# Old x loaded ahead of the last weights, old x pieces moved between jobs and end, column sums ahead of the cache transposes, plain weights split earlier

## The reference

```python
def swiglu_half(x, pre_g, w_gate, w_up, w_down, post_g):
    h = rms_norm(x, pre_g)
    u = jax.nn.silu(h @ w_gate) * (h @ w_up)
    return x + 0.5 * rms_norm(u @ w_down, post_g)

def run_layer(x, pos, token_mix, ff1, mix, ff2):
    x = swiglu_half(x, *ff1)
    mo, proj = mixer_projections(rms_norm(x, mix_pre_g), pos, w_in, ...)
    h_m, attn, new_state = token_mix(proj)      # mLSTM heads and latent attention
    ...
    x = x + rms_norm(merged @ w_out, mix_post_g)
    return swiglu_half(x, *ff2), new_state
```

## Time and profile before

| | |
|---|---|
| time, median of 3 runs | 1250.32 us (1250.29 to 1253.73) |
| the profiled execution | 1250.35 us, of which the span (first to last instruction) 1248.6 |
| TensorE matmuls busy | 1188.5 us (95%) |
| VectorE busy | 929.9 us (74%) |
| ScalarE busy | 639.2 us (51%) |
| GpSimd busy | 99.7 us (8%) |
| mean granted TensorE clock | 0.982 of 2.4 GHz |
| chain that ended last | PE 78%, DVE 11%, issue 4%, ACT 4%, DMA 2% |

### The profile page before, as it was taken

How to read it: one execution, slowest core, us unless ns; L and a number is a source line. 1 busy time by engine, 2 the same in 40 slices (tenths; PEclk the granted TensorE clock), 3 DMA queues, 4 the chain that set the end, 5 groups by cost and what they waited for, 6 DMA issues and landing times.

```text
span 1248.6 us, 22101 instructions
## 1 busy us (share of the span) xinstructions
PE 1188.5 (95%) x8460; PEld 1126.8 (90%) x8460; DVE 929.9 (74%) x1394; ACT 639.2 (51%) x1250; POOL 99.7 (8%) x128
## 2 busy tenths in 40 slices
PE   6999999999989999999998999999999999999877
PEld 6999999999989799999965679989999999999876
DVE  7988999899888734644357551279889998998856
ACT  5565655565555423132266443345666555655544
POOL 2000000000000003604034001110000000000000
PEclk8999999999999899999999999999999999999989
DMA  8224224313323312423200001232242243133222
GB/s 254 69 68 136 68 84 121 102 56 115 102 76 131 90 51 68 92 55 91 76 14 24 24 1 35 68 110 68 69 135 69 85 119 102 59 112 102 77 102 76
DMA packets 162549, 104.72 MB, mean 84 GB/s; under 512 B 16907, under 2 KB 160352, under 8 KB 161936
## 3 DMA queue, kind: packets, MB, share of 16 engines
q1 hardware_dynamic: 161344, 101.50, 28.2%
q0 software_dynamic: 1088, 1.84, 0.5%
q10 hardware_dynamic: 16, 0.00, 0.0%
HBM read 95.06 MB, written 8.27 MB: 83 GB/s over the span
## 4 chain that ended last, share of the span: by engine, by line
PE 78%; DVE 11%; issue 4%; ACT 4%; DMA 2%; SPq 0%; DVEq 0%; POOL 0%; ACTq 0%
PE PS L641 43%; PE PS L391 17%; PE PS L683 4%; ACT WQ_HI L740 3%; PE PS L409 2%; PE PS L2250 2%; PE PS L2221 2%; DVE SB L787 2%; PE PS L2236 1%; DMA RAWP<-in_ff_w_up 1%; DVE TU L866 1%; DVE SB L791 1%; DVE UF L1068 1%; PE PS L1944 1%; PE PS L1596 1%
## 5 line engine op out<-in xcount | busy, mean ns | idle before, releaser
L641 PE MATMUL PS<-HHI,WQ_HI 128*128 128x288 f32 x1120 | 332.8, 297 | 8.0 <-ACT SNQ L722 3.9
L641 PE MATMUL PS<-HLO,WQ_HI 128*128 128x288 f32 x1120 | 331.1, 296 | 0.0
L641 PE MATMUL PS<-HHI,WQ_LO 128*128 128x288 f32 x1120 | 330.0, 295 | 0.0
L641 PEld LDWEIGHTS PS<-HHI,WQ_HI 128*128 128x128 f32 x1120 | 210.2, 188 | 10.9 <-ACT WQ_HI L740 6.6
L740 ACT ACTIVATE WQ_HI<-SB 128x512 fp32r<-128x512 f32 (+2 forms) x288 | 163.9, 571 | 105.2 <-PE PS L641 60.2
L641 PEld LDWEIGHTS PS<-HHI,WQ_LO 128*128 128x128 f32 x1120 | 211.2, 189 | 0.0
L641 PEld LDWEIGHTS PS<-HLO,WQ_HI 128*128 128x128 f32 x1120 | 210.4, 188 | 0.0
L641 PE MATMUL PS<-UHI,WQ_HI 128*128 128x288 f32 x616 | 187.2, 304 | 11.8 <-DVE ULO L853 9.3
L641 PE MATMUL PS<-ULO,WQ_HI 128*128 128x288 f32 x616 | 184.3, 299 | 0.0
L641 PE MATMUL PS<-UHI,WQ_LO 128*128 128x288 f32 x616 | 184.3, 299 | 0.0
L740 ACT ACTIVATE WQ_HI<-RAWP 128x512 fp32r<-128x512 f32 (+2 forms) x216 | 121.7, 564 | 41.0 <-PE PS L641 34.2
(11 more groups left out here) (384 smaller groups left out, 2164.9 us busy)
## 6 DMA issues: line engine op xcount, KB each, us to landing
RAWP<-in_ff_w_gate SPq DMA_DIRECT2D x44, 512.0 KB, 4.0
RAWP<-in_ff_w_up SPq DMA_DIRECT2D x44, 512.0 KB, 5.3
RAWP<-in_ff_w_down SPq DMA_DIRECT2D x24, 768.0 KB, 4.4
RAW<-in_w_in SPq DMA_DIRECT2D x21, 512.0 KB, 3.8
x_spill<-X SPq DMA_DIRECT2D x2, 2304.0 KB, 9.2
XOLD<-x_spill SPq DMA_DIRECT2D x2, 2304.0 KB, 9.7
RAWP<-in_ff_w_down SPq DMA_DIRECT2D x8, 512.0 KB, 3.4
RAW<-in_w_out SPq DMA_DIRECT2D x8, 512.0 KB, 4.0
```

Of the source, the lines that this page charges most:

```text
L641: last = nc.tensor.matmul(PS[:, bank, 0:HT], w, h, start=i in (P1, P7, P2) and k == 0 and s == 0, stop=k == n - 1 and s == 2, skip_group_c ...
```

## The change

Four edits:

1. In `ffn_sp` the load of XOLD is issued behind the weights of the last job but one, and so ahead of the last job's; its wait for the last gate product goes with it.
2. Six old x pieces stay inside the last three jobs, two in each, in other places. Pieces 6 to 9 move behind the jobs, into bank 4: 6, 7 and 8 between the transposes of y, 9 into `finish_pe`; their copies move in ScalarE's order accordingly.
3. At the end of the first FFN the column sums go ahead of the cache transposes, with six fill instructions in front and none between; ScalarE takes the root ahead of the cache's copies; VectorE does the two weight splits ahead of the reciprocal and the cache's low part behind the last H_LO.
4. Three of the second FFN's four first plain splits move: two on ScalarE behind the seventh output of the out projection, the third in front of the root; on VectorE all three ahead of the reciprocal.

```diff
@@ post_dve
             nc.vector.reciprocal(INV[:], ROOT[:]).then_inc(e["inv"].sem, 1)
-            plain_low(dve, ff[1], 0, 1)
-            plain_low(dve, ff[1], 1, 0)
             dve.wait_ge(e["spread"].sem, 1 + e["spread"].base)
@@ ffn_sp
                 if r == 1:
                     spill_x()
-            sp.wait_ge(*f["used"].at(nth_product(GJOB[JF - 1], P3)))
-            sp.wait_ge(*f["moved"].at(16))
-            sp.dma_start(XOLD[:].rearrange("p k t -> p (k t)"), spill).then_inc(f["moved"].sem, 16)
+                if r == NJ - 2:
+                    sp.wait_ge(*f["used"].at(nth_product(GJOB[JF - 1], P3)))
+                    sp.wait_ge(*f["moved"].at(16))
+                    sp.dma_start(XOLD[:].rearrange("p k t -> p (k t)"), spill).then_inc(f["moved"].sem, 16)
@@ ffn_pe, ffn_act
-        OLD_PIECES = {0: {P2: 0, P5: 1, P4: 2, P1: 3}, 1: {P2: 4, P5: 5, P4: 6, P1: 7}, 2: {P2: 8, P5: 9}}
+        OLD_PIECES = {0: {P4: 0, P1: 1}, 1: {P2: 2, P4: 3}, 2: {P2: 4, P4: 5}}
@@ fpost_act
             if p is fpost[1]:
-                old_copied(act, 2 * TT - 2)
-                old_copied(act, 2 * TT - 1)
+                for n in (6, 7):
+                    old_copied(act, n)
             y_square(act, f, p, KD // 2 - 1, 1)
             y_square(act, f, p, KD // 2 - 1, 0)
             if p is fpost[1]:
                 y_scaled(act, p, KD - 1)
                 y_scaled(act, p, KD - 2)
+                old_copied(act, 8)
             if p is fpost[0]:
                 split_hi_first(act)
+            post_act(act, p)
+            if p is fpost[0]:
                 cache_act(act)
-            post_act(act, p)
+            if p is fpost[1]:
+                old_copied(act, 9)
@@ fpost_dve
-            dve.wait_ge(*e["root"].at(1))
-            nc.vector.reciprocal(INV[:], ROOT[:]).then_inc(e["inv"].sem, 1)
             if p is not None:
                 split_lo(dve, MIX0)
                 split_lo(dve, MIX0 + 1)
-                cache_dve(dve)
+            dve.wait_ge(*e["root"].at(1))
+            nc.vector.reciprocal(INV[:], ROOT[:]).then_inc(e["inv"].sem, 1)
...
                 low_dve(dve, p, KD - 1)
+                cache_dve(dve)
@@ fpost_pe
             if p is fpost[0]:
-                keep_busy(7, 8)
-                cache_pe(pe)
-                keep_busy(1, 2)
+                keep_busy(1, 6)
             if p is fpost[1]:
-                for t, k0, k1 in ((0, 0, 6), (2, 0, 6), (1, 0, 6)):
-                    new_turned(pe, t, k0, k1)
+                old_turned(pe, 6)
+                new_turned(pe, 0, 0, 6)
+                old_turned(pe, 7)
+                new_turned(pe, 2, 0, 6)
+                new_turned(pe, 1, 0, 6)
+                old_turned(pe, 8)
             pe.wait_ge(*p["acc"].at(KD - 1))
             frame_sums(ACC[:], sum_bank(p), True, True).then_inc(p["sum"].sem, 1)
             if p is fpost[0]:
-                keep_busy(1, 1)
+                cache_pe(pe)
                 pe.wait_ge(*p["inv"].at(1))
@@ old_turned
-        OLD_BANKS = (6, 7)
+        OLD_BANKS = (6, 7, 6, 7, 6, 7, 4, 4, 4, 4)
...
-            if n >= 2:
-                pe.wait_ge(o["old_copied"], n - 1)
+            if n == 6:
+                pe.wait_ge(*ff[1]["ev11"].at(NJ - NPLAIN))
+                pe.wait_ge(*ff[1]["snap"].at(3 * (NJ - NPLAIN)))
+            elif n >= 2:
+                pe.wait_ge(o["old_copied"], n - 1 if n < 6 else n)
@@ out_act
                 if m + 2 < KD:
                     split_hi(act, B_OUT + m + 2)
+                elif m + 2 == KD:
+                    plain_high(act, ff[1], 0, 0)
+                    plain_high(act, ff[1], 0, 1)
@@ the order of ScalarE and of VectorE
             out_act(act, post)
-            plain_high(act, ff[1], 0, 0)
+            plain_high(act, ff[1], 1, 0)
             post_act(act, post)
-            plain_high(act, ff[1], 0, 1)
-            plain_high(act, ff[1], 1, 0)
...
             plain_low(dve, ff[1], 0, 0)
+            plain_low(dve, ff[1], 0, 1)
+            plain_low(dve, ff[1], 1, 0)
             post_dve(dve, post)
```

More of the change, by code:

```diff
@@ L978, in ffn_act @@
                         y_scaled(act, p, 2 * q - 1)
-                old = OLD_PIECES.get(r - URGENT - 1, {}) if f is ff[1] and r + 1 < NJ else {}
+                old = OLD_PIECES.get(r - URGENT - 1, {}) if f is ff[1] else {}
                 weight_hi(act, f, r + 1, P5)
-                if old:
+                if P2 in old:
                     old_copied(act, old[P2])
                 weight_hi(act, f, r + 1, P4)
-                if old:
-                    old_copied(act, old[P5])
                 if r + 1 not in SOLO:
                     snap(act, f, r + 1, 0)
-                    if old:
+                    weight_hi(act, f, r + 2, P1)
+                    if P4 in old:
                         old_copied(act, old[P4])
-                    weight_hi(act, f, r + 2, P1)
-                    if old:
+                    if P1 in old:
                         old_copied(act, old[P1])
@@ L1352, in old_turned @@
             c, rows = FRAMES[t]
-            bank = OLD_BANKS[n % 2]
+            bank = OLD_BANKS[n]
             if n == 0:
                 pe.wait_ge(*ff[1]["moved"].at(32))
-            if n >= 2:
-                pe.wait_ge(o["old_copied"], n - 1)
+            if n == 6:
[3 more added lines that the diff above has]
+                pe.wait_ge(o["old_copied"], n - 1 if n < 6 else n)
             for k in range(4):
@@ L1366, in old_copied @@
             act.wait_ge(o["old_T"], n + 1)
-            nc.scalar.activation(XTOK[0:rows, t, 4 * P * h:4 * P * (h + 1)], PS[0:rows, OLD_BANKS[n % 2], :],
+            nc.scalar.activation(XTOK[0:rows, t, 4 * P * h:4 * P * (h + 1)], PS[0:rows, OLD_BANKS[n], :],
                                  ACT.Copy).then_inc(o["old_copied"], 1)
@@ L1384, in new_turned @@
             if t == 2 and k0 == 0:
-                pe.wait_ge(o["old_copied"], 2 * TT)
+                pe.wait_ge(o["old_copied"], 6)
             if t >= 3:
@@ L1397, in finish_pe @@
                 new_turned(pe, t, 6, KD)
+            old_turned(pe, 9)
             for t in range(3, TT):
```

## The result

The changed kernel took 1235.63 us (median of 4 runs, 1233.92 to 1238.98), the kernel before beside it 1251.78 (4 runs, 1250.29 to 1253.73): a ratio of 0.987, with a 95% interval of 0.985 to 0.990. The profiled execution took 1234.87, with a span of 1233.1.

A forecast was written before the change was run, and what follows sets the result against it. TensorE, busy 95% of the span, was taken as the bound, with gains only where it waits, runs slow or does removable work. -12.0 + 1.9 - 6.0 - 0.6 = -16.7 took 1250.35 to 1233.7 us; range 1231.0 to 1238.6.

The forecast's parts named there:

- the likeliest case: Whole kernel: all parts of the change work as forecast, 16.7 us faster, at 1233.7 us; chance 0.68.
- the rival with the clock fall: End of first FFN: the clock falls after all, so that part gives 4.3 and the kernel takes 1235.4; chance 0.14.
- Old x ahead of the last weights: Second FFN's last down jobs: earlier load removes wait and low clock, four pieces leave; 12.0 us faster, between 11.5 and 12.4.
- the lower of the two ways: Last down jobs: gain worked out from the first FFN's four jobs plus six pieces, 1222.4 against 1233.9, or 11.5 us.
- Four pieces at the end: Behind the last down jobs: ScalarE's copies ahead of the last two squares make these 1.9 us later, between 1.5 and 2.9.
- The 0.4 for drain and handover: Behind the last down jobs: an estimated 0.4 us on top of 2.0 for two pieces and two copies.
- Column sums ahead: End of first FFN: scaling of X 4.3 us earlier; 6.0 us gained if TensorE keeps its clock, 4.3 if not.
- Plain weights: End of out projection: no split left behind the reciprocal, 0.6 us gained, between 0 (fill sets it) and 1.1.
- ScalarE's copies: Last down jobs: rival that ScalarE or VectorE sets their pace, each of three jobs losing a piece-wait; 1237 us, chance 0.11.
- the last weights, now behind the load: Last down jobs: rival that the old x load delays the last weights, at worst 1.6 us; slower kernel, chance 0.02.
- that rival: Last down jobs: load no earlier, SyncE held by its wait for the gate product; 1243.8 us, chance 0.03.

The follow-up runs named there:

- e2: Kernel before with only the first-seam change (column sums ahead of the cache transposes, six fill instructions ahead of them): median 1246.29 us, ratio 0.998.
- e3: Kernel before with only the plain-weight splits of the out projection moved: one run, 1248.39 us.
- e11: Changed kernel once more, unaltered: 1238.20 us (6 runs), ratio 0.990.
- e1: Kernel before with only the old x part (earlier load, six pieces inside the jobs, four at the end): 1241.11 us, ratio 0.991.
- e5: Changed kernel with one fill instruction for six ahead of the column sums at the end of the first FFN: 1240.52 us.
- e6: Changed kernel with one fill instruction for five behind the spread at the end of the first FFN: 1238.84 us.
- e7: Changed kernel with the last squares ahead of copies 6 to 9 on ScalarE, and pieces 7 to 9 behind the sums on TensorE: 1235.18 us.
- e9: Changed kernel with three fill instructions for five behind the third seam's spread and none between its groups of sums: 1243.53 us.
- e4: Changed kernel with the old x load alone put back behind the last weights: 1245.89 us (12 runs).
- e8: Changed kernel with six fill instructions in TensorE's 4.65 us wait ahead of the last four down jobs, both FFNs: 1233.96 us.
- e10: Changed kernel with the edits of e7, e8 and e9 joined: 1230.35 us (6 runs, 1226.70 to 1240.30).
- e12: Changed kernel with the edits of e7 and e8 joined, third seam left as changed: 1229.73 us, ratio 0.985.

## Why the prediction was right, and where it was not

The forecast of 1233.7 is 1.9 below the measured 1235.63, which lies in the range, and the likeliest case came. The time alone doesn't tell that: 1235.63 is nearer to the 1235.4 of the rival with the clock fall, and only the trace of the profiled execution, at 1.00 in the tile behind the first seam, rules that out. That the forecast came so near is in part luck: over all ten runs the median, 1237.1, is 3.4 above it. By its steps:

- **Old x ahead of the last weights, -12.0.** Right in mechanism: 15.2 us ahead and no wait. In size, the jobs took 48.65 to 50.05 with the old order (before, e2, e3; mean 49.5) and 37.31 to 38.70 with the new (changed, e11, e1, e5, e6, e7, e9; mean 38.0): 11.5, the lower of the two ways that the prediction worked out. The difference between the two profiles that are shown, 12.63, has 1.1 of chance in it.
- **Four pieces at the end, +1.9.** Measured +1.87 to +1.92, squares at 2.47 where 2.45 was worked out. The 0.4 for drain and handover, an estimate that no row gave, came out as 0.43 (2.47 less the 2.04 of two pieces and two copies). e7 shows that their place in the queues of ScalarE and TensorE is all of it.
- **Column sums ahead, -6.0.** This is the step that failed in part. 4.3 was right, sums and scaling 3.87 and 7.73 behind the last product. The other 1.7, "if TensorE keeps its clock", was put down to the edit, but the old seam keeps its clock too in two of its three profiles (e1, e3), and the new one in all nine. On these the edit can claim about 0.5 in the mean, a third of the 1.5 that the fall cost, and three profiles are few. The pair of profiles shows 5.77 only because the one shown fell. Taking the clock of one execution as a property of the code was the error; the rival of 4.3 came out right in size, without its fall.
- **Plain weights, -0.6.** Measured -0.72, as e3.
- **Sum.** With the measured terms -11.5 + 1.9 - 4.3 - 0.7 = -14.6, about what the runs give (16.2 in the first comparison, 14.8 in the second, 14.1 over all ten runs). The prediction's -16.7 was 2 too much.

Of the rivals, ScalarE's copies appear in no wait of TensorE inside the jobs, and the last weights, now behind the load, held nobody up. The load was early, so that rival did not come; its price was wrong all the same. It left 1.8 of the first part, but e4, where the load is late, keeps 5.2, as the later pieces also shorten the wait.

The Trainium skill, TensorE: Matmul & The Clock Gate (Part 1, on the clock gate), says that the number of slow matmuls at the start of a kernel varies from run to run. The trace shows the like inside a kernel: behind the same wait the jobs of FFN1 took 34.71 and 35.82 in the changed kernel's two profiles.

## What to carry to other kernels

A load that waits in an in-order queue behind one that waits for its buffer is late by that buffer's time (15.2 us here); issue it ahead when its own condition is met earlier, and price the wait together with the slow clock behind it. Work moved out of a busy stretch to the end of a kernel must stand behind the chain that ends it, in each engine's queue, or the chain pays for it. Before a clock fall is booked as a gain of an edit, look for it in a second profile of the same code.

## What the runs showed of the hardware that was not expected

- The same waits are followed by a fall of the granted clock in some executions and not in others: 1.16 and 1.30 us in the old first seam (fell once in three), 1.94 us early in FFN2 (ten in fourteen), holes of 0.22 and 0.55 us (once in two). The wait of 1.94 us stands early in FFN1 too, and there it fell in one of fourteen (e8). Behind the wait of 4.65 us it fell all 22 times (eleven profiles, two FFNs: 0.50 to 0.64 over the first 4 us). Fill in that wait kept it at 1.00 in all three kernels that have it (e8, e10, e12).
- The mix stage, the same code in all of them, took from 361.35 to 369.64 us, and its clock makes the difference. In every profile it is near 0.50 around 685, for about 7 us in ten, 14 in three (e5, e6, e10) and 24 in e9; in eight (e2, e4, e5, e7 to e11) it also falls near 625. The stage took 361.4 to 361.7 without the second fall, 361.9 to 363.2 with it, 364.4 (e6), 366.0 (e5, e10) and 369.6 (e9). The 8.0 of e9 is more than the whole first seam gave.
